# A transformer block with 32 experts on one core: q and k both made before the shift is known, their pages' fixes, and six smaller moves

## The reference

```python
mod = (silu(c) @ w_ada + b_ada)          # six rows of 1024: sh1, sc1, gt1, sh2, sc2, gt2
h = rmsnorm(x, g_pre_mix) * (1 + sc1) + sh1
q, k, v, z = split(h @ w_in)             # 512, 512, 512 and 2 x 512 columns
y_a = chunk_attention(q, k, v, rel_bias) # 8 heads, chunks of 64
y_b = spatial_gating(z, ...)             # gelu, layernorm of one half, 128x128 causal matmuls
g_a, g_b = split(sigmoid(h @ w_gate + b_gate))
y = rmsnorm((g_a * (y_a @ w_branch_a) + g_b * (y_b @ w_branch_b)) @ w_out, g_post_mix)
x = x + gt1 * y
h = rmsnorm(x, g_pre_ffn) * (1 + sc2) + sh2
logits = h @ w_router + b_router         # 32 experts, the top 4 of each token, softmax of their logits
act = min(g, 7) * sigmoid(1.702 * min(g, 7)) * (clip(l, -7, 7) + 1)   # g, l = halves of h @ w_gate_up[e] + b_gate_up[e]
y = sum over the chosen e of gate * (act @ w_down[e] + b_down[e])
x = x + gt2 * rmsnorm(y, g_post_ffn)
```

## Time and profile before

| | |
|---|---|
| median of 3 runs | 1183.96 us (1181.68 to 1184.78) |
| the profiled execution, its own time | 1179.82 us |
| its span, first to last instruction | 1177.6 us |
| mean granted TensorE clock | 0.954 |
| TensorE busy | 1029.8 us (87%) |
| VectorE, ScalarE, GpSimd busy | 294.7, 179.7, 31.6 us |
| read from memory | 462.50 MB, 395 GB/s over the span |

### The profile page before, as it was taken

The page is one execution under the profiler, slowest core; times in us unless marked ns, Lnnn a source line. Parts: engine busy times, 40 slices in busy tenths (PEclk is TensorE's granted clock), DMA queues, the critical chain, the costliest instruction groups (busy, mean ns, idle before and its releaser), DMA issues.

```text
span 1177.6 us, 21864 instructions
## 1 busy us (share of the span) xinstructions
PE 1029.8 (87%) x8300; PEld 500.5 (43%) x8301; DVE 294.7 (25%) x813; ACT 179.7 (15%) x453; POOL 31.6 (3%) x54
## 2 busy tenths in 40 slices
PE   4999999977788999899979898989898989797965
PEld 3847887433342343334333433343334333333322
DVE  4636664242111221112111211121112111111112
ACT  3213340221111111101110111011101110101002
POOL 1001002210000000000000000000000000000000
PEclk9999999978899999999999999999999999798988
DMA  9899835989999999999999999999999999999994
GB/s 351 322 384 379 336 119 209 425 356 425 422 426 421 429 425 425 426 381 427 425 424 427 424 426 425 427 426 425 424 426 425 426 426 425 426 425 425 425 425 197
DMA packets 61484, 464.91 MB, mean 395 GB/s; under 512 B 5900, under 2 KB 10060, under 8 KB 28568
## 3 DMA queue, kind: packets, MB, share of 16 engines
q1 hardware_dynamic: 51808, 397.45, 81.7%
q10 hardware_dynamic: 9320, 66.11, 13.5%
q0 software_dynamic: 336, 1.07, 0.3%
HBM read 462.50 MB, written 2.11 MB: 395 GB/s over the span
## 4 chain that ended last, share of the span: by engine, by line
PE 58%; DMA 27%; DVE 4%; SPq 3%; issue 3%; ACT 2%; ACTq 1%; POOL 0%; DVEq 0%
PE pp L1537 21%; DMA arena<-in_w_down_dram 12%; PE pp L1568 11%; DMA bgu<-in_b_gate_up_dram 9%; PE pp L1323 5%; DMA arena<-in_w_gate_up_dram 4%; PE pp L1501 4%; PE pp L1245 3%; PE pp L1336 2%; PE pp L1255 2%; PE po L1398 2%; PE pp L1510 2%; PE po L1482 2%; SPq L374 1%; DMA arena<-in_w_ada_dram 1%
## 5 line engine op out<-in xcount | busy, mean ns | idle before, releaser
L1537 PE MATMUL pp<-arena,work 128*32 128x256 f32 (+1 forms) x3840 | 388.7, 461 | 42.9 <-ACT work L709 41.0
L1537 PEld LDWEIGHTS pp<-arena,work 128*32 128x32 f32 (+1 forms) x3840 | 167.1, 121 | 248.6 <-issue 142.0
L1568 PE MATMUL pp<-arena,work 128*32 128x256 f32 (+1 forms) x1920 | 194.5, 442 | 28.8 <-DMA arena<-in_w_down_dram 21.6
L1089 DVE TENSOR_SCALAR work<-pp 128x128 f32<-128x128 f32 (+1 forms) x74 | 24.9, 337 | 441.8 <-PE pp L1537 441.8
L1568 PEld LDWEIGHTS pp<-arena,work 128*32 128x32 f32 (+1 forms) x1920 | 77.2, 118 | 128.2 <-issue 82.4
L1501 PE MATMUL pp<-h_sb,work 128*32 128x256 f32 (+1 forms) x480 | 68.0, 490 | 37.7 <-DMA bgu<-in_b_gate_up_dram 18.1
L712 ACT ACTIVATE work<-work 128x128 f32<-128x128 f32 (+1 forms) x74 | 25.9, 350 | 419.3 <-DVE work L1089 419.3
L1482 PE MATMUL po<-work 64*128 64x512 f32 x304 | 75.5, 615 | 1.2 <-ACT work L728 1.2
L1083 DVE COPY work<-pp 128x256 f32<-128x256 f32 (+1 forms) x37 | 19.4, 525 | 211.4 <-PE pp L1501 211.4
L1323 PE MATMUL pp<-arena 128*128 128x256 f32 x256 | 57.1, 382 | 0.0
L1501 PEld LDWEIGHTS pp<-h_sb,work 128*32 128x32 f32 (+1 forms) x480 | 22.4, 125 | 79.3 <-issue 48.8
(11 more groups left out here) (224 smaller groups left out, 602.6 us busy)
## 6 DMA issues: line engine op xcount, KB each, us to landing
arena<-in_w_gate_up_dram SPq DMA_DIRECT2D x128, 2048.0 KB, 32.1
arena<-in_w_down_dram SPq DMA_DIRECT2D x32, 2048.0 KB, 36.2
arena<-in_w_down_dram ACTq DMA_DIRECT2D x62, 1024.0 KB, 13.8
arena<-in_w_ada_dram SPq DMA_DIRECT2D x11, 2048.0 KB, 14.1
arena<-in_w_in_dram SPq DMA_DIRECT2D x4, 2048.0 KB, 19.6
arena<-in_w_gate_dram SPq DMA_DIRECT2D x4, 2048.0 KB, 13.2
arena<-in_w_out_dram SPq DMA_DIRECT2D x2, 2048.0 KB, 10.3
arena<-in_w_ada_dram SPq DMA_DIRECT2D x2, 1024.0 KB, 13.2
```

The source lines that it names most:

```text
L1537: mm = t_.matmul(pp[j * m:(j + 1) * m, UP[hh], 0:w].rearrange("p (s f) -> p s f", s=2), hgT[:, at:at + m], gu_w[slot][:, k, :, r * PAIR:(r ...
L1568: mm = t_.matmul(pp[j * m:(j + 1) * m, UP[0], 0:w], actT[:, at:at + m], wd[:, j * w:(j + 1) * w], start=(n == 0), stop=(n == KD - 1))
```

## The change

It has these parts.

1. The page of k is loaded right behind that of q, ahead of row 0 of mod, and vv ahead of ada 2. q and k are both made from hT without the shift. The eight one-column matmuls of row 0 stand inside k's second half; their result becomes mix_shift by a copy on ScalarE. hT is made with the shift behind k, for v.
2. VectorE builds the fix of k as it did that of q, eight more instructions. SP waits for s_qfix twice: 1 ahead of page 7 (vv), which takes q's slot, 2 ahead of page 8 (ada 2 first half), which takes k's.
3. x is loaded first of the large transfers. Rows 1 and 0 of mod, q and k are loaded in parts by rows; 30 matmuls of spin stand where 8 stood.
4. b_down is loaded later in SP's stream, behind two quarters of w_gate_up; the two last pages of the mixer don't wait for it any more.
5. GpSimd still multiplies by the scale, but ScalarE's 1/rms and GpSimd's shift are gone: 1/rms is a factor in the selection matrices, and the shift is added when hgT is copied out of PSUM, which VectorE now does. The columns of h are taken in pairs, as those of the weights are, so that shift_col fits hgT.
6. Ahead of the experts' loop the load of expert 0's dhi goes ahead of dlo of expert 1, and doesn't wait for the spill of x1.
7. The last expert's dhi is issued by SyncE in its queue, ahead of x1_back, and no longer by ScalarE.

The diff, cut to its core:

```diff
-PAGES = [("dve", "ada", 1, 0), ("dve", "ada", 1, 1), ("pe", "q", 0, 0), ("dve", "ada", 0, 0), ("dve", "ada", 0, 1)]
-PAGES += [("pe", "k", 0, 0), ("pe", "v", 0, 0), ("dve", "ada", 2, 0), ("pe", "vv", 0, 0), ("dve", "ada", 2, 1)]
+PAGES = [("dve", "ada", 1, 0), ("dve", "ada", 1, 1), ("pe", "q", 0, 0), ("pe", "k", 0, 0), ("dve", "ada", 0, 0)]
+PAGES += [("dve", "ada", 0, 1), ("pe", "v", 0, 0), ("pe", "vv", 0, 0), ("dve", "ada", 2, 0), ("dve", "ada", 2, 1)]
...
+HALVES, TAIL = ((0, 2), (2, 4)), ((0, 2), (2, 3), (3, 4))
+PARTS = {0: HALVES, 1: TAIL, 2: ((0, 4), (4, 8)), 3: ((0, 4), (4, 8)), 4: HALVES, 5: TAIL}
...
+                if n - RING in (page_of("q"), page_of("k")):
+                    sp.wait_ge(s_qfix, n - RING - page_of("q") + 1)
...
             load_gu(1, 1, 2)
+            sp.wait_ge(s_zero, 2)
+            for j in range(2):
+                sp.dma_start(y_sb[j * TB:j * TB + NEXP, :],
+                             b_down[0][:, j * 512:(j + 1) * 512]).then_inc(s_bd, 16)
...
+            sp.wait_ge(s_ug, 2 * TT)
+            sp.wait_ge(s_hm, 2 * TT)
+            sp.wait_ge(s_lg, TT)
+            for r in range(2):
+                load_dhi(sp, 0, r)
             sp.wait_ge(s_spill, 16 * TT)
...
             sp.wait_ge(s_y, sp.snap(done, min_val=1, max_val=NEXP * NBLK))
+            for r in range(2):
+                load_dhi(sp, last_e, r)
...
-                for half in range(2):
-                    cols = slice(half * 512, half * 512 + 512)
-                    pool.wait_ge(s_hr, 2 * t + half + 1)
-                    g.tensor_tensor(h_sb[:, t, cols], h_sb[:, t, cols], shift[:, cols], ALU.add).then_inc(s_h2, 1)
...
+            evac(heads(kT, 0), ACT.Copy)
+            act.wait_ge(s_proj, bank + 1)
+            a.copy(mix_shift, pp[:, bank % 4, 0:KD]).then_inc(s_projev, 1)
+            bank += 1
...
             for k in (0, 1, 2, 3, 6, 7):
-                act.wait_ge(s_mixcol, 3 if k < KD // 2 else 4)
                 a.activation(hT[:, k, :], xT_bank(k), ACT.Identity, scale=mix_scale[:, k:k + 1],
                              bias=mix_shift[:, k:k + 1]).then_inc(s_hTa, 1)
...
-                    act.wait_ge(s_turn, it)
-                    a.copy(hgT[:, 0:w], pp[:, TURN, 0:w]).then_inc(s_turned, 1)
...
+            dve.wait_ge(s_ssx, 1)
+            v.reciprocal(rstd[:, 0:2], rms[:, 0:2]).then_inc(s_xr, 1)
             page_sum(1, 0, range(4))
...
+            dve.wait_ge(s_projev, 4)
+            def shift_rows(name, at, ks):
+                grid = acc[:, 1, at:at + AW]
+                for k in ks:
+                    w_k = page_k(page_of(name), k)
+                    if k == 0:
+                        ins = v.tensor_scalar(grid, w_k, mix_shift[:, k:k + 1], None, ALU.mult)
+                    else:
+                        ins = v.scalar_tensor_tensor(out=grid, in0=w_k, scalar=mix_shift[:, k:k + 1], in1=grid,
+                                                     op0=ALU.mult, op1=ALU.add)
...
+            shift_rows("q", 0, range(2))
+            dve.wait_ge(s_proj, 5)
             for k in (4, 5):
                 v.tensor_scalar(hT[:, k, :], xT_bank(k), mix_scale[:, k:k + 1], mix_shift[:, k:k + 1],
                                 ALU.mult, ALU.add).then_inc(s_hTv, 1)
...
+            shift_rows("q", 0, range(2, KD))
+            shift_rows("k", AW, range(KD))
             modulation(2)
...
+                dve.wait_ge(s_turn, it)
+                shifts = shift_col.rearrange("p (j i a) -> p i j a", i=w // P, a=1).to_broadcast([P, w // P, P // m, m])
+                v.tensor_tensor(hgT[:, 0:w].rearrange("p (i j a) -> p i j a", i=w // P, a=m),
+                                pp[:, TURN, 0:w].rearrange("p (i j a) -> p i j a", i=w // P, a=m), shifts,
+                                ALU.add).then_inc(s_turned, 1)
...
-                    ins = v.tensor_scalar(sel[:, t, :], places, rank[:, t, e], None, ALU.is_equal)
+                    ins = v.tensor_scalar(sel[:, t, :], places, rank[:, t, e], rstd[:, 6 + t:7 + t], ALU.is_equal,
+                                          ALU.mult)
...
-            spin(2)
+            spin(8)
...
-            spin(6)
+            spin(22)
```

More of the change, by code:

```diff
@@ L747, in _ @@
                 place(n)
+            place(NEXP - 1)
             a.preload_act_table(ACT.Sqrt)
@@ new lines, in page_T @@
+                banks = [next_bank()]
+                columns = next_bank() if name == "k" else None
+                banks.append(next_bank())
+                for kh in range(2):
+                    rows_landed(pe, pg, 4 * kh)
+                    for m in range(KA):
+                        if kh and m == 2 and name == "k":
+                            shift_columns(columns)
+                        for k in range(4 * kh, 4 * kh + 4):
+                            if m == 0 and name == "q":
+                                hT_there(k, False)
+                            mm = t_.matmul(banks[m // 2][:, m % 2 * TOK:(m % 2 + 1) * TOK],
+                                           page_k(pg, k)[:, m * P:(m + 1) * P], hT[:, k, :],
+                                           start=(k == 0 and m % 2 == 0), stop=(k == KD - 1), skip_group_check=True)
+                        if kh and m % 2:
+                            mm.then_inc(s_proj, 1)
```

203 lines of the change are left out of this document (86 added, 117 removed).

## The result

| | before | after |
|---|---|---|
| median (lowest to highest) | 1182.64 us (1178.29 to 1184.78), 12 runs | 1190.12 us (1183.87 to 1193.73), 12 runs |
| ratio, 95% interval | | 1.007 [1.0056, 1.0085] |
| profiled execution, its own time | 1179.82 us | 1193.1 us |
| span, mean granted clock | 1177.6 us, 0.954 | 1191.1 us, 0.933 |

The change makes the kernel slower by 0.7%; the forecast was no change, and the range ended at 1188.5. The profiled execution of after is one of the long ones of its twelve (13.3 us above that of before), so shifts in its trace add up to more than the 7.5 us between the medians. Line 1274 is q and k now, L1288 v and vv, L1259 u, L1230 a row of mod, L1321 the spatial matmuls; in the loop L1530 gathers the rows, L1566 is w_gate_up, L1597 w_down, L1088 the copy to hgT.

A forecast was written before the change was run, and what follows sets the result against it. The prediction took the experts' loop as bound by its bytes and TensorE as busy throughout 113 to 234 us. Its terms, +3.9 - 0.8 + 0.1 - 3.3 = -0.1 us, gave a median of 1183.9 us, range 1177.0 to 1188.5.

The forecast's parts named there:

- The bound: Experts' loop: bound by its bytes at 421 to 429 GB/s, so longer or shorter instructions in it cost nothing.
- The term for the loop: Experts' loop: the hgT copy and selection add 0.1 us a block, hidden but for the first block; +0.1 us.
- The start: Up to the spatial matmuls: they come at 116.6, not 112.67 us; +3.9 us, ends -0.4 and +5.6.
- Start of q: First stretch: q starts at 21.7 us, not at 24.43, 2.7 us ahead.
- k's end: Behind q: k follows at once, takes 14.05 us and ends at 51.9 us, against 56.96 before.
- Behind the start: From 113 to 234 us: TensorE has no free time, so nothing of the delay is caught up.
- b_down and expert 0's dhi: Loads ahead of the loop: moving them brings nothing, since both slots are full until the loop frees them.
- The router: Ahead of the loop: without ScalarE's part, L1045 comes earlier; -0.8 us, between 0 and -1.1.
- The last expert: End of kernel: last w_gate_up quarter lands 4.9 us earlier, w_down's last steps wait for dhi; -3.3 us, 0 to -4.9.
- C: Rival at the start: spins take 0.515 us each, q starts at 27.5 us; +5.8 us, 1189.7 us; chance 0.16.
- B: Rival at the start: pages land in time, TensorE keeps its 4.1 us lead; 1175.9 us; chance 0.20.
- D: Rival at the end: moving the last dhi load gains nothing, that term is 0; 1187.2 us; chance 0.14.

The follow-up runs named there:

- wide_pad3: Kernel before with three useless matmuls (0.7 us) ahead of w_gate_up in each wide block of the experts' loop: 1184.95 us, 1.0037 of before.
- after_spin30: Changed kernel with 30 in place of 22 useless matmuls behind the transposes of x: 1187.53 us, 1.0054 of before.
- tail_bdown: Kernel before with the last expert's dhi in SyncE's queue and b_down loaded behind two quarters of w_gate_up: 1178.24 us, 0.9975 of before.
- tail_only: Kernel before with only the last expert's dhi issued by SyncE behind dlo, ahead of x1_back: 1177.60 us, 0.9974 of before.
- spin30_halffix: after_spin30 with four of eight instructions left out in each fix of q and k, which alters the routing: 1192.82 us, 1.0081 of before.
- dve_warm8: dve_copy with eight useless matmuls ahead of the wait for w_down's upper half in every narrow block: 1187.77 us, 1.0065 of before.
- dve_copy: Kernel before with only the copy to hgT moved from ScalarE to VectorE: 1186.15 us, 1.0038 of before.
- head_only: Kernel before with parts 1 to 3 alone (page order, q and k without the shift, loads in parts, 30 spins): 1188.75 us, 1.0064 of before.
- norm_only: Kernel before with parts 5 and 6 alone (norm in the selection, shift and hgT copy on VectorE, expert 0's dhi first): 1185.48 us, 1.0032 of before.

## Why the prediction was wrong

**The bound.** "An instruction that gets shorter or longer in it costs nothing while its block is done before the next weights are" is the step that failed. Slices at 421 to 429 GB/s were read as a bound by bytes with TensorE free beside it. The one slice of 381, named in the prediction and passed over, was the place where TensorE was the bound already: SyncE had waited 35.4 us there for w_gate_up's matmuls. wide_pad3 shows the price with nothing else changed: 9.8 us of TensorE's time cost 4.4, where this step says 0. The term for the loop was +0.1; parts 5 and 6 measure +3.8, with the router's gain of 0.8 in it, so the loop's part is about +4.6.

**The start.** Start of q: right within half a microsecond. k's end: wrong by 5.0 us, of which 4.5 are the clock (32.6 for 28.1). The prediction had seen k take 15.77 us and took 14.05 "without the pause"; but there was a pause ahead of q now, since the spins, at 0.234 us each, ended at 17.9 and VectorE's sums at 20.5. VectorE's fixes, the wait of SyncE, ada 3 and the reciprocal followed in the order forecast, 4.0 to 5.8 us late, and row 3 started when VectorE released it, at 109.1 for 104.8. TensorE's waits came otherwise: 2.91 us ahead of row 2, where none had been forecast, and 0.26 us ahead of row 3. The term was +3.9, its upper end +5.6; the trace shows +7.7. With the clock kept (after_spin30) it shows +4.5.

**Behind the start.** "Nothing is caught up" is right: +7.7 at the spatial matmuls, +7.0 at the start of the loop with the router's gain.

**b_down and expert 0's dhi.** Part 4 is worth nothing, as said (tail_bdown). Part 6 had no run of its own; parts 5 and 6 with the copy's cost taken off leave -0.7, which the router explains.

**The router.** Right. L1047 (L1045 before) comes 6.46 us behind the first sum with w_out's result (249.33 - 242.87) where it was 7.28 (242.40 - 235.12): -0.8.

**The last expert.** Right: -3.3 forecast, -3.1 measured. The last quarter of w_gate_up did land earlier. Time from issue to landing (median) of the quarters issued behind 1100 us, of before and of tail_only, and the last block's w_gate_up in tail_only:

```profile
arena<-in_w_gate_up_dram SPq DMA_DIRECT2D x2, 2048.0 KB, 47.4
```

```profile
arena<-in_w_gate_up_dram SPq DMA_DIRECT2D x2, 2048.0 KB, 42.6
...
1146.83 8.80 PE L1541 MATMUL pp<-arena,work 128*32 128x256 f32 x128 [0.46 <-ACT work L712]
```

They come 4.8 us sooner, as forecast (4.9), and these 128 matmuls no longer wait for the last quarter: they end at 1155.6, and in before at 1159.1. The order of issue did set the order of the bytes. The Trainium skill's sentence (DMA: Bandwidth & Descriptors, Issuing engines are not separate DMA queues), by which the choice of the engine saves issue time only, would have made this 0. Of the last block in after, TensorE:

```profile
1177.84 1.93 PE L1597 MATMUL pp<-arena,work 128*32 128x256 f32 x32 [0.37 <-issue]
```

It doesn't wait for dhi, which had landed by then: 19.3 us after its issue at 1157.50. That it would wait was forecast and is not so in after; in tail_only the gap there is 0.93 us in place of 0.37, so dhi can have cost 0.6 us there.

**The rivals.** C gave 1189.7, near what came, by a mechanism that is false: the spins took 0.234 us, not 0.515. That it came near is luck. B fell, and not by the clock alone: with q's clock kept (after_spin30) the spatial matmuls still come 4.5 us later than in before. D fell with tail_only.

## What to carry to other kernels

Ask of a loop whose DMA rate looks flat not whether it is bound by bytes but where in it each side waits; one slice under the plateau can be where compute is the bound. A pad of known length tells: here 0.7 us in each wide block was paid in full in the steady part and by just under half over the whole kernel. A faster step ahead of a wait that stays is no gain, and on TensorE it can be a loss: here the wait grew, and the lower clock came more often in what followed. Of a step that is brought forward, look for the next wait of TensorE that it runs into and take the prices of both clock levels for the matmuls behind it. The best kernel here is the one with the fewest edits: part 7 alone, 0.9974 of before.

## What the runs showed of the hardware

- 1.96 us without work and 16 one-column matmuls ahead of q were followed by 112 matmuls in 27.2 us, and with the pause filled by eight more matmuls of no use in 24.4 (after_spin30 and spin30_halffix).
- The clock also fell with no wait at all ahead of it, behind 16 one-column matmuls (16 of 128x256 in 5.39 us, in after and in after_spin30). In spin30_halffix the same 16 stood there and it did not fall (3.70 us), so they are not enough to make it fall.
- A mean granted clock of 0.958 went with 1187.8 us (dve_warm8) and one of 0.942 with 1186.2 (dve_copy): a mean that is raised by added matmuls says nothing of the time.
- One load of 2 MB moved from ScalarE's queue to SyncE's, behind the loads that stand there, let those land 4.8 us sooner (42.6 us from issue in tail_only, 47.4 in before).
- One execution differs from the next by as much as the parts measured here: the profiled ones of after, head_only and norm_only lie 3.0, 4.8 and 3.7 us over the median of their kernel.
